# MLA queries' rotary columns of all heads in two blocks, halves swapped by a TensorE product and rotated on VectorE; keys' rotary part spread by one DMA

## What is computed

```python
def apply_rope(t, cos, sin):
    t1, t2 = jnp.split(t, 2, axis=-1)
    return jnp.concatenate([t1 * cos - t2 * sin, t1 * sin + t2 * cos], axis=-1)

def mla_attention(c_q, c_kv, k_rope, q_norm_g, w_uq, kv_norm_g, w_ukv, cos, sin):
    q = (rms_norm(c_q, q_norm_g) @ w_uq).reshape(b_, l_, MLA_HEADS, QK_NOPE + QK_ROPE)   # 8 heads, 64 + 32
    q_nope, q_rope = jnp.split(q, [QK_NOPE], axis=-1)
    q_rope = apply_rope(q_rope, cos[:, None, :], sin[:, None, :])
    kv = (rms_norm(c_kv, kv_norm_g) @ w_ukv).reshape(b_, l_, MLA_HEADS, QK_NOPE + V_DIM)
    k_nope, v = jnp.split(kv, [QK_NOPE], axis=-1)
    k_rope = apply_rope(k_rope, cos, sin)
    k = jnp.concatenate([k_nope, jnp.broadcast_to(k_rope[:, :, None, :], ...)], axis=-1)
    ...   # scores of each head, mask, softmax, product with v
```

## Time and profile before

| | |
|---|---|
| median of 3 runs | 880.22 us (879.47 to 880.50) |
| the profiled execution's own time | 879.67 us |
| its span, first to last instruction | 878.0 us |
| PE busy | 864.3 us (98%) |
| DVE busy | 600.1 us (68%) |
| ACT busy | 426.5 us (49%) |
| POOL busy | 109.3 us (12%) |
| granted clock of PE, mean | 0.998 |

### The profile page before, as it was taken

The page is one execution under the profiler, slowest core; times in us unless marked ns, Lnnn a source line. Parts: engine busy times, 40 slices in busy tenths (PEclk is TensorE's granted clock), DMA queues, the critical chain, the costliest instruction groups (busy, mean ns, idle before and its releaser), DMA issues.

```text
span 878.0 us, 14120 instructions
## 1 busy us (share of the span) xinstructions
PE 864.3 (98%) x5938; PEld 793.7 (90%) x5938; DVE 600.1 (68%) x841; ACT 426.5 (49%) x613; POOL 109.3 (12%) x102
## 2 busy tenths in 40 slices
PE   8999999999999999999999999999999999999996
PEld 7998899998888988879999988889987899999885
DVE  5899997688586674796555554587986765555445
ACT  5745363456654874435444443246553554444320
POOL 0443430122004121011000000021100200000000
PEclk9999999999999999999999999999999999999999
DMA  9964666664356752557665656377544756565531
GB/s 288 276 182 104 190 171 182 176 176 129 92 157 201 232 168 72 168 155 235 187 191 179 185 190 192 121 248 219 167 136 133 237 181 191 183 181 189 192 120 48
DMA packets 117944, 154.18 MB, mean 176 GB/s; under 512 B 7455, under 2 KB 93882, under 8 KB 117850
## 3 DMA queue, kind: packets, MB, share of 16 engines
q1 hardware_dynamic: 116154, 148.31, 55.7%
q0 software_dynamic: 1728, 4.98, 1.8%
HBM read 151.44 MB, written 1.05 MB: 174 GB/s over the span
## 4 chain that ended last, share of the span: by engine, by line
PE 86%; DVE 10%; DMA 2%; ACT 1%; issue 0%; SPq 0%; DVEq 0%
PE acc L589 24%; PE acc L590 24%; PE acc L591 24%; DVE conv L1789 3%; DVE w_lo L1634 3%; PE acc L673 2%; PE acc L676 2%; PE acc L674 2%; DMA staged<-in_w_in 1%; PE misc L757 1%; PE acc L627 1%; DVE rope_t L1750 1%; PE misc L1010 1%; DMA x<-in_x 1%; ACT w_hi L1215 0%
## 5 line engine op out<-in xcount | busy, mean ns | idle before, releaser
L1634 DVE TENSOR_TENSOR w_lo<-staged,w_hi 128x1024 fp32r<-128x1024 f32 (+1 forms) x274 | 333.4, 1237 | 153.2 <-ACT w_hi L1215 152.3
L589 PE MATMUL acc<-x_hi,w_hi 128*128 128x256 f32 (+2 forms) x1288 | 365.9, 284 | 1.3 <-DVE w_lo L1634 1.3
L590 PE MATMUL acc<-x_lo,w_hi 128*128 128x256 f32 (+2 forms) x1288 | 363.7, 282 | 0.0
L591 PE MATMUL acc<-x_hi,w_lo 128*128 128x256 f32 (+2 forms) x1288 | 361.1, 280 | 0.0
L1215 ACT CAST w_hi<-staged 128x1024 fp32r<-128x1024 f32 (+1 forms) x274 | 278.5, 1045 | 92.4 <-DMA staged<-in_ffn_w_down 45.8
L589 PEld LDWEIGHTS acc<-x_hi,w_hi 128*128 128x128 f32 x1288 | 241.6, 188 | 3.3 <-issue 2.5
L591 PEld LDWEIGHTS acc<-x_hi,w_lo 128*128 128x128 f32 x1288 | 243.8, 189 | 0.0
L590 PEld LDWEIGHTS acc<-x_lo,w_hi 128*128 128x128 f32 x1288 | 242.1, 188 | 0.7 <-issue 0.2
L589 PE MATMUL acc<-w_hi,h_hi 128*128 128x512 f32 (+1 forms) x176 | 67.0, 381 | 0.0
L590 PE MATMUL acc<-w_lo,h_hi 128*128 128x512 f32 (+1 forms) x176 | 66.9, 380 | 0.0
L591 PE MATMUL acc<-w_hi,h_lo 128*128 128x512 f32 (+1 forms) x176 | 66.9, 380 | 0.0
(11 more groups left out here) (392 smaller groups left out, 1155.1 us busy)
## 6 DMA issues: line engine op xcount, KB each, us to landing
staged<-in_ffn_w_gu SPq DMA_DIRECT2D x88, 512.0 KB, 3.6
staged<-in_w_in SPq DMA_DIRECT2D x58, 512.0 KB, 3.8
staged<-in_ffn_w_down SPq DMA_DIRECT2D x44, 512.0 KB, 3.5
staged<-in_gla_w_in SPq DMA_DIRECT2D x24, 512.0 KB, 4.4
staged<-in_moba_w_in SPq DMA_DIRECT2D x24, 512.0 KB, 4.5
staged<-in_w_o SPq DMA_DIRECT2D x8, 512.0 KB, 3.8
staged<-in_gla_w_out SPq DMA_DIRECT2D x8, 512.0 KB, 3.7
staged<-in_moba_w_out SPq DMA_DIRECT2D x8, 512.0 KB, 3.6
```

The lines of the kernel that those rows point to most:

```text
L589: pe.matmul(dst, st_hi, mv_hi, start=start, stop=False)
L590: pe.matmul(dst, st_hi, mv_lo, start=False, stop=False)
L591: return pe.matmul(dst, st_lo, mv_hi, start=False, stop=stop)
L1634: nc.vector.tensor_tensor(lo, raw, hi, ALU.subtract).then_inc(split, 1)
```

## The change

- The columns of `w_uq` come into SBUF in another order: first the 32 rotary columns of all eight heads (256 columns, two blocks of 128), then the 64 unrotated ones of each (four blocks of 128). The one DMA becomes four, two for each half of the contraction, with runs of 128 and of 256 bytes in DRAM; they stand between the slots 9 and 16 instead of between 3 and 4.
- On PE the queries are 12 products with 128 columns (three banks) instead of 16 with 96. One more product (`qs`) swaps the halves of all heads' rotary columns by a block-diagonal permutation of 128x128, on 512 rows, between `kn3` and `vt0`.
- On ACT the first bank (both rotary blocks) is one copy to `q_rope`, which lies on `sq_cq`; the other two banks are two copies each.
- The rotation is three DVE operations on 128x512, in slot 18 behind the tap there. POOL's 12 operations and the two DMAs to `q_swap` are gone. Four DMAs from POOL bring the rotated rows to `qT` (`q_spread`), and one brings the rotated keys to the eight heads of `kT` in place of the eight copies.
- The tables `cos`, `sin` and `swap` fill all 128 partitions; the constants' second load is 96 columns wider.
- ACT's wait ahead of `gate_sc` is for `sc_ready`. DVE waits for `q_spread` before the first gated output, since `m` lies on `q_rope`.
- On ACT the rounding of the third pair of MLA's heads stands one step earlier, ahead of the last `probsT`.

```diff
-MISC += ["uq%d" % _i for _i in range(4)] + ["kn%d" % _i for _i in range(4)] + ["vt%d" % _i for _i in range(3)]
+MISC += ["uq%d" % _i for _i in range(3)] + ["kn%d" % _i for _i in range(4)] + ["qs"] + ["vt%d" % _i for _i in range(3)]
...
-            sp.dma_start(w_uq[:], d["w_uq"][0].rearrange("(c p) n -> p c n", p=P)).then_inc(s["mla_loaded"], 16)
...
-            z_slots(8, COUNT["z"])
+            z_slots(8, 10)
+
+            for c in range(2):
+                uq = d["w_uq"][0][c * P:c * P + P, :].rearrange("p (h e) -> p h e", h=HEADS)
+                for i, (c0, e0, e1) in enumerate(((0, NOPE, QK), (HEADS * ROPE, 0, NOPE))):
+                    sp.dma_start(w_uq[:, c, c0:c0 + HEADS * (e1 - e0)].rearrange("p (h e) -> p h e", h=HEADS),
+                                 uq[:, :, e0:e1]).then_inc(s["mla_loaded"], 16)
+                    z_slots(10 + 2 * (2 * c + i), 12 + 2 * (2 * c + i))
+            z_slots(18, COUNT["z"])
...
-            for j in range(4):
+            for j in range(3):
                 b = open_bank("uq%d" % j)
                 for i in range(2):
                     for c in range(2):
-                        mm = pe.matmul(b[0:QK, i * ROWS:(i + 1) * ROWS], w_uq[:, c, (2 * j + i) * QK:(2 * j + i + 1) * QK],
+                        mm = pe.matmul(b[:, i * ROWS:(i + 1) * ROWS], w_uq[:, c, (2 * j + i) * P:(2 * j + i + 1) * P],
                                        cq_z[:, c, :], start=c == 0, stop=c == 1)
...
+            await_read(pe, "uq0")
+            filled(pe.matmul(open_bank("qs"), cst("swap", P), q_rope, start=True, stop=True), "qs")
...
-                    for j in range(4):
+                    await_full(act, "uq0")
+                    nc.scalar.copy(q_rope, bank("uq0")).then_inc(read_sem("uq0"), 1)
+                    for j in (1, 2):
                         await_full(act, "uq%d" % j)
-                        nc.scalar.copy(qT[0:QK, 2 * j:2 * j + 2, :], bank("uq%d" % j)[0:QK, :]
-                                       .rearrange("p (h r) -> p h r", h=2)).then_inc(read_sem("uq%d" % j), 1)
+                        for i in range(2):
+                            last = nc.scalar.copy(qT[0:NOPE, 4 * j - 4 + i:4 * j:2, :], bank("uq%d" % j)[i * NOPE:(i + 1) * NOPE, :]
+                                                  .rearrange("p (h r) -> p h r", h=2))
+                        last.then_inc(read_sem("uq%d" % j), 1)
...
+            def rotate_queries():
...
+                await_full(dve, "qs")
+                read(nc.vector.tensor_tensor(t, bank("qs").rearrange("p (c r) -> p c r", c=2), table("sin"), ALU.mult), "qs")
+                link(nc.vector.tensor_tensor(q, q, table("cos"), ALU.mult))
+                await_read(dve, "qs")
+                nc.vector.tensor_tensor(q, q, t, ALU.add).then_inc(s["q_roped"], 1)
...
+                if sl.at == 18:
+                    rotate_queries()
...
-            for j in range(4):
-                rotate(qT, q_swap, rope, j, rope_t, cst("cos", KEYS, rope)[:, META:], cst("sin", KEYS, rope)[:, META:],
-                       s["q_roped"], j + 1)
+            pool.wait_ge(s["q_roped"], 1)
+            for g in range(4):
+                pool.dma_start(qT[NOPE:QK, g:HEADS:4, :], sq_cq[g * ROPE:(g + 1) * ROPE, :, :]).then_inc(s["q_spread"], 16)
...
-            for i in range(HEADS):
-                last = nc.gpsimd.tensor_copy(kT[NOPE:QK, i, :], kr_t[NOPE:QK, :])
-            last.then_inc(s["k_spread"], 1)
...
+            pool.dma_start(kT[NOPE:QK, :, :], kr_t[NOPE:QK, :].unsqueeze(1).to_broadcast([ROPE, HEADS, KEYS])
+                           ).then_inc(s["k_spread"], 16)
```

More of the change, by code:

```diff
@@ L130 @@
 for _name, _n in [("ident", P), ("ones", P), ("mask_mla", S0 + S1), ("mask_moba", P + ROWS), ("cos", KEYS),
-                  ("sin", KEYS), ("swap", ROPE), ("inv_freq", 1), ("sign", 1)]:
+                  ("sin", KEYS), ("swap", P), ("inv_freq", 1), ("sign", 1)]:
     CONST[_name] = CONST_N
@@ L154, in constants @@
     ang = (np.arange(KEYS, dtype=np.float32)[None, :] * inv[:, None]).astype(np.float32)
-    rope = slice(NOPE, NOPE + ROPE)
-    put("cos", rope, np.concatenate([np.cos(ang), np.cos(ang)]).astype(np.float32))
-    put("sin", rope, np.concatenate([-np.sin(ang), np.sin(ang)]).astype(np.float32))
+    for g in range(P // ROPE):
+        rope = slice(g * ROPE, (g + 1) * ROPE)
+        put("cos", rope, np.concatenate([np.cos(ang), np.cos(ang)]).astype(np.float32))
+        put("sin", rope, np.concatenate([-np.sin(ang), np.sin(ang)]).astype(np.float32))
     swap = np.roll(np.eye(ROPE, dtype=np.float32), ROPE // 2, axis=1)
-    put("swap", slice(0, ROPE), swap)
-    put("swap", rope, swap)
+    put("swap", every, np.kron(np.eye(P // ROPE, dtype=np.float32), swap))
     inv2 = np.power(np.float32(500000.0), -np.arange(0, 32, 2, dtype=np.float32) / np.float32(32)).astype(np.float32)
@@ L378, in hybrid_stack @@
         m_rows, meta_h = flat_gates[0:META, 0:DM], flat_gates[0:META, DM:2 * DM]
+        q_rope = sq_cq[:].rearrange("p c r -> p (c r)")
         pos_i = kr_t[0:ROPE, 0:ROWS].bitcast(I32)
@@ L880, in _ @@
             pe.wait_ge(s["conf_split"], 1)
-            pe.wait_ge(s["q_roped"], 4)
-            pe.wait_ge(s["k_spread"], 1)
+            pe.wait_ge(s["q_spread"], 64)
+            pe.wait_ge(s["k_spread"], 16)
             def mla_scores(i):
@@ L1316, in take_gates @@
                          bias=gate_bias(b, 2 * i + 1))
-            act.wait_ge(s["q_roped"], 4)
+            act.wait_ge(s["sc_ready"], 1)
             await_read(act, "vec")
@@ L1374, in _ @@
                              bias=gate_bias("mla", 2 * b + 1))
+                if n == HEADS + 1:
+                    mla_u_hi(2)
                 if n >= 2:
@@ L1385, in _ @@
                     mla_u_hi((n - 6) // 2)
-            mla_u_hi(2)
             mla_u_hi(3)
@@ L1820, in two_heads, with table @@
                 return a.unsqueeze(1).to_broadcast([ROPE, 2, ROWS])
+            def rotate_queries():
+                def table(name):
+                    return cst(name, KEYS)[:, META:].unsqueeze(1).to_broadcast([P, 2, ROWS])
+                q, t = [a.rearrange("p (c r) -> p c r", c=2) for a in (q_rope, rope_t[:])]
+                await_full(dve, "qs")
[3 more added lines that the diff above has]
+                nc.vector.tensor_tensor(q, q, t, ALU.add).then_inc(s["q_roped"], 1)
             def rotate_keys():
-                dve.wait_ge(s["q_roped"], 4)
+                dve.wait_ge(s["q_roped"], 1)
                 await_full(dve, "krs")
@@ L1930, in _ @@
                     conv_taps(23 + sl.index // 2, 24 + sl.index // 2)
+            dve.wait_ge(s["q_spread"], 64)
             for before, b in (("sc", "pool"), ("pool", "conf")):
@@ L2323, in link @@
                 pool.wait_ge(pool_chain, chained[0])
-            def rotate(dst, swap, rows, j, tmp, cos, sin, done, number):
-                hs = slice(2 * j, 2 * j + 2)
-                t = tmp[rows, :].rearrange("p (h r) -> p h r", h=2)
-                nc.gpsimd.tensor_tensor(t, swap[rows, hs, :], sin.unsqueeze(1).to_broadcast([ROPE, 2, ROWS]), ALU.mult)
-                link(nc.gpsimd.tensor_tensor(dst[rows, hs, :], dst[rows, hs, :], cos.unsqueeze(1).to_broadcast([ROPE, 2, ROWS]),
-                                             ALU.mult))
-                nc.gpsimd.tensor_tensor(dst[rows, hs, :], dst[rows, hs, :], t, ALU.add).then_inc(done, 1)
-                pool.wait_ge(done, number)
             nc.gpsimd.memset(ssq[:], 0.0).then_inc(s["cleared"], 1)
@@ L2368, in _ @@
             pool.wait_ge(s["sc_ready"], 1)
-            for j in range(4):
-                await_read(pool, "uq%d" % j)
-            a, b = slice(NOPE, NOPE + ROPE // 2), slice(NOPE + ROPE // 2, QK)
-            pool.dma_start(q_swap[a, :, :], qT[b, :, :]).then_inc(s["q_swapped"], 16)
-            pool.dma_start(q_swap[b, :, :], qT[a, :, :]).then_inc(s["q_swapped"], 16)
-            pool.wait_ge(s["tables_loaded"], 16)
-            rope = slice(NOPE, QK)
-            pool.wait_ge(s["q_swapped"], 32)
-            for j in range(4):
-                rotate(qT, q_swap, rope, j, rope_t, cst("cos", KEYS, rope)[:, META:], cst("sin", KEYS, rope)[:, META:],
-                       s["q_roped"], j + 1)
+            pool.wait_ge(s["q_roped"], 1)
+            for g in range(4):
+                pool.dma_start(qT[NOPE:QK, g:HEADS:4, :], sq_cq[g * ROPE:(g + 1) * ROPE, :, :]).then_inc(s["q_spread"], 16)
             pool.wait_ge(s["kr_roped"], 1)
-            for i in range(HEADS):
-                last = nc.gpsimd.tensor_copy(kT[NOPE:QK, i, :], kr_t[NOPE:QK, :])
-            last.then_inc(s["k_spread"], 1)
-            pool.wait_ge(s["k_spread"], 1)
+            pool.dma_start(kT[NOPE:QK, :, :], kr_t[NOPE:QK, :].unsqueeze(1).to_broadcast([ROPE, HEADS, KEYS])
+                           ).then_inc(s["k_spread"], 16)
+            pool.wait_ge(s["k_spread"], 16)
             pool.wait_ge(s["sc_split"], 1)
```

9 lines of the change are left out of this document (3 added, 6 removed).

## The result

The changed kernel takes 874.79 us (median; 874.34 to 877.89), the kernel before 879.97 us on the same chip: ratio 0.9946, 95% interval 0.9934 to 0.9959. That is 5.2 us less; 2.3 were forecast, and 877.0 was the low end of the range. The direction was right, the size was not.

What follows compares the result with a forecast made beforehand. PE was busy for 98% of the span, so only fewer or shorter products or its few waits could save time. -0.87 + 0.2 - 1.6 = -2.3 us gave 877.4 to 877.9, rounded to 878.0 us; range 877.0 to 879.7.

Steps and rivals of the forecast that it cites:

- The queries' products: On PE, twelve query products take 5.18 us and the swap 0.86, instead of 6.91 us: -0.87 us, at least 0.51 saved.
- The new wait on PE: On PE, the swap waits for ACT's copies of `kn0`: +0.2 us, between 0 and 0.6; rival of 1 to 1.5, chance 0.08.
- DVE and POOL: Without POOL's rotation DVE's taps take 5.6 us, so PE's waits at slots 24 and 26 go: -1.6 us; lag-stays rival 0.16.
- Edits at nothing: The DMAs spreading queries and keys, ACT's earlier release before `gate_sc` and the moved rounding were all taken to change nothing.
- The loads: `w_uq`'s four DMAs on SP were taken at 0; rival: they delay the weight ring, 884.5 us, chance 0.04.
- rival: Three: the lag stays, 879.5 us (0.16); small loads delay the ring, 884.5 (0.04); ACT holds the swap longer, 879.0 (0.08).

Runs made afterwards that it cites:

- e4_before_no_rotation: The kernel before, with POOL's 12 operations of the queries' rotation left out (four writes of 8 columns instead, queries unrotated): 878.30 us, ratio 0.9988.
- e2_before_pad384: The kernel before, with 384 bytes per SBUF partition left empty ahead of the region holding the later stages' operands: 877.04 us, ratio 0.9968.
- the undisturbed execution: The changed kernel profiled again with no edit, without the drop of PE's clock: profiled execution 874.48 us, median 874.99 us, ratio 0.9951.
- e8_ring_256: The changed kernel with 256 bytes left empty ahead of the weights' rings, all tiles moving along: 875.61 us, ratio 0.9951.
- e12_loads_old_place: The changed kernel with w_uq's four DMAs issued together where its one DMA stood, ahead of w_ukv: 876.70 us, ratio 0.9965.

## Why the prediction was right in direction and wrong in size

**The queries' products.** Right: 5.18 us for the 12, as taken. The swap takes 1.03 us, not 0.86. The query product was the wrong row to size it by; the value products of the same 512 rows at 0.98 were the nearer one. -0.17 us of the saving.

**The new wait on PE.** The mechanism was right (the copies of `kn0` hold the swap), the size not: ACT's two copies of a bank take 1.17 us where I counted two of 0.48, keys and wait take 2.31 us instead of 2.12. Products and wait together give -0.32 us in place of -0.67.

**DVE and POOL.** Right: -1.59 us against -1.6, the taps 5.6 us, the rest of slot 24 ends (85.92) 13 us before PE wants it, three rotation operations in 2.0 us (I had 2.2). `e4_before_no_rotation` gives this term by itself. What the prediction could not see is how little the kernel before was tied to it: 0.9 us of the 1.6 also go if DVE's taps happen to run ahead of POOL's first operation, as in `e2_before_pad384`.

**Edits at nothing.** Right for the spreads: the queries' four DMAs are issued at 89.37 and the keys' one, from 104.46, is done by 110.9. POOL alone waits for the latter, 5.88 us ahead of a memset, and PE waits for nothing of POOL's behind it.

**The loads.** 0 was right, since the pieces are spread. My argument for it (they overlap as `w_ukv`'s do) was not the reason: the same four in one place cost 1.7 us. Spread out, each held SP for 0.6 to 1.2 us, where I had allowed up to 2.3.

**The step that failed** is the one that the sum does not have. "The constants' second load is 96 columns wider" stands in the list of the change, and the prediction has no term for it. It moved every later tile by 384 bytes, to the ring's remainder modulo 256 bytes, and so took 0.005 us off each of 737 distances in five stages: 3.6 us, or 2.75 us when the waits that grew are counted against it; the kernels that make and undo only this moved by 3.0 us (with the part at slots 24 and 26) and 2.9 us. No rival covered it, and the range's low end of 877.0 had no term for anything behind 118 us. The sentence that closes the prediction looked in the right view for the wrong thing: it said that a gain over 3 us would mean unseen waits in PE's distances, and here the products themselves came closer.

The sum by what was measured: -0.32 - 1.59 - 2.75 = -4.66 us of 5.24; of the other 0.6 us, 0.38 stand from 118 to 245 us. There `e4_before_no_rotation` alone gains 0.15 and `e2_before_pad384` alone 0.19, so most of this belongs to the same two causes. The remaining 0.2 us stay unexplained.

## What to carry to other kernels

When a diff changes the size of any tile that is placed by a running cursor, list what moves with it, and compare start distances in stages that the diff doesn't touch: 0.005 us in each of 737 products was more here than PE's waits for `w_lo`. Before a gain is put down to an algorithm, run the old kernel with only the placement of the new one. Where small DMAs replace a large one, try their place in the issuing queue: here the same four cost 1.7 us in one place and nothing that shows when spread.

## What the runs showed of the hardware that I had not expected

- A product of 512 columns starts 0.2267 us after the one before if the stationary block and the moving operand differ by 0 modulo 256 bytes in their place in a partition, and 0.232 to 0.233 us if by 64 or 128. That holds where products of 512 columns follow one another; these are the differences that were tried, and why it is so is not shown. For products of 256 columns the distance also depends on placement (0.1183 to 0.1200 us), but by another rule, which these runs leave open.
- Between DVE and POOL, a run of instructions of one can hold the other off, or the two can alternate: in one kernel POOL's first operation, 1.47 us in the other, stood for 6.55 us until DVE's 14 taps and a rest were through; in the other 12 of the 14 taps took 1.43 us each instead of 0.40, in turn with POOL's 12 operations. The Trainium skill, "SBUF — State Buffer", "Who interferes with whom", says that the two exclude each other for a whole instruction, and the traces agree: a tap that waits for one of POOL's operations lasts 1.51 us instead of 0.48. What they add is that one operation can be held off over a whole run of the other's.
- PE's granted clock can fall to 0.50 (1.2 GHz) once more after its first rise: in the changed kernel's first profile from 13.0 to 19.8 us, in that of `e8_ring_256` from 12.0 to 15.4. The other profiles do not show it. Windows of the changed kernel's first profile (us, busy time and count of PE, PEld, DVE, ACT, POOL, granted clock, DMA):

```profile
10.00:12.00 2.00, 0.77 (x5) 0.55 (x6) 1.93 (x7) 1.50 (x3) 0.00 (x0) 1.00 1.07 354
12.00:14.00 2.00, 2.00 (x11) 1.53 (x12) 1.97 (x4) 1.34 (x3) 0.00 (x0) 0.75 1.06 400
14.00:16.00 2.00, 2.00 (x10) 1.42 (x9) 1.45 (x4) 1.81 (x3) 0.00 (x0) 0.50 1.20 279
```

Ahead of it PE did 5 products from 10 to 12 us, where it did 10 in the undisturbed execution; but 7 in `e12_loads_old_place` left the clock at 1.00, and with 8 in this stretch it fell in `e8_ring_256` and stayed in the kernel before. So this does not settle the cause.
